# First scale and first gate of the modulation as dot products on VectorE instead of products on TensorE, in a one-core transformer kernel

## What is computed

```
sc   = silu(c)                                     # 1024 numbers
mod  = sc @ w_mod + b_mod                          # 6 vectors of 1024
sh1, s1, g1, sh2, s2, g2 = split(mod, 6)
h    = rms_norm(x, norm1_g) * (1 + s1) + sh1       # x: 256 tokens x 1024
u, gate = split(h @ w_pw1 + b_pw1, 2)
u    = dwconv(u * sigmoid(gate)) + b_dw            # width 31, in segments of 64 tokens
u    = silu(layer_norm(u)) @ w_pw2 + b_pw2
x    = x + g1 * u
x    = x + g2 * (relu((rms_norm(x) * (1 + s2) + sh2) @ w1)**2 @ w2)
...                                                # final norm, two attention layers
```

## Time and profile before

| | before |
|---|---|
| median of 3 runs | 1031.82 us (1031.65, 1031.82, 1034.67) |
| profiled execution, its own time | 1034.53 us |
| its span, first to last instruction | 1032.7 us |
| TensorE busy | 1002.6 us, 97% |
| VectorE busy | 603.2 us, 58% |
| ScalarE busy | 506.6 us, 49% |
| mean granted TensorE clock | 0.994 of full |

### The profile page before, as it was taken

The page is one execution under the profiler, slowest core; times in us unless marked ns, Lnnn a source line. Parts: engine busy times, 40 slices in busy tenths (PEclk is TensorE's granted clock), DMA queues, the critical chain, the costliest instruction groups (busy, mean ns, idle before and its releaser), DMA issues.

```text
span 1032.7 us, 13807 instructions
## 1 busy us (share of the span) xinstructions
PE 1002.6 (97%) x5782; PEld 843.5 (82%) x5782; DVE 603.2 (58%) x730; ACT 506.6 (49%) x639; POOL 23.7 (2%) x47
## 2 busy tenths in 40 slices
PE   8998999999998999999999999999999999999996
PEld 6665779999997999878888888889988788888885
DVE  3587355444447639955555455764796655545465
ACT  4443455444555545654444444554565643444453
POOL 0000000000000000000000000000000100000000
PEclk9999999999999999999999999999999999999998
DMA  9967597555505544046555555436233554555531
GB/s 344 418 254 285 212 379 255 214 186 188 211 22 191 215 145 164 27 155 221 200 182 185 202 172 211 165 126 236 90 115 123 176 210 175 203 171 196 191 115 42
DMA packets 30648, 195.57 MB, mean 189 GB/s; under 512 B 3571, under 2 KB 5672, under 8 KB 9592
## 3 DMA queue, kind: packets, MB, share of 16 engines
q1 hardware_dynamic: 30586, 194.68, 52.0%
HBM read 193.61 MB, written 2.04 MB: 189 GB/s over the span
## 4 chain that ended last, share of the span: by engine, by line
PE 82%; DVE 11%; issue 3%; ACT 3%; DMA 1%; POOL 0%; DVEq 0%; SPq 0%; POOLq 0%; ACTq 0%
PE ps L1593 58%; PE ps L1968 9%; PE ps L2024 5%; DVE lo L1048 3%; ACT hi L588 1%; PE ps L1698 1%; PE ps L2272 1%; PE ps L2154 1%; PE ps L2108 1%; DVE scratch L1385 1%; DVE scratch L1451 1%; PE ps L1715 1%; PE ps L1777 1%; DVE scratch L1402 1%; DMA h<-x 0%
## 5 line engine op out<-in xcount | busy, mean ns | idle before, releaser
L1048 DVE TENSOR_TENSOR lo<-raw,hi 128x2048 fp32r<-128x2048 f32 (+5 forms) x140 | 310.3, 2219 | 234.8 <-ACT hi L588 234.7
L588 ACT ACTIVATE hi<-raw 128x2048 fp32r<-128x2048 f32 (+4 forms) x140 | 263.8, 1888 | 127.0 <-PE ps L1593 105.5
L1593 PE MATMUL ps<-hi,xh 128*128 128x512 f32 (+2 forms) x704 | 276.3, 392 | 9.3 <-DVE xl L1089 4.3
L1593 PE MATMUL ps<-lo,xh 128*128 128x512 f32 (+2 forms) x704 | 269.7, 383 | 0.0
L1593 PE MATMUL ps<-hi,xl 128*128 128x512 f32 (+2 forms) x704 | 269.4, 383 | 0.0
L1593 PEld LDWEIGHTS ps<-hi,xh 128*128 128x128 f32 x704 | 132.4, 188 | 46.3 <-issue 14.2
L1593 PEld LDWEIGHTS ps<-lo,xh 128*128 128x128 f32 x704 | 132.4, 188 | 25.2
L1593 PEld LDWEIGHTS ps<-hi,xl 128*128 128x128 f32 x704 | 132.7, 189 | 22.3
L1593 PE MATMUL ps<-hi,gh 128*128 128x512 f32 (+2 forms) x328 | 125.1, 382 | 0.0
L1593 PE MATMUL ps<-lo,gh 128*128 128x512 f32 (+2 forms) x328 | 124.6, 380 | 0.0
L1593 PE MATMUL ps<-hi,gl 128*128 128x512 f32 (+2 forms) x328 | 124.6, 380 | 0.0
(11 more groups left out here) (248 smaller groups left out, 1063.2 us busy)
## 6 DMA issues: line engine op xcount, KB each, us to landing
raw<-stream SPq DMA_DIRECT2D x142, 1024.0 KB, 4.9
scratch<-stream SPq DMA_DIRECT2D x22, 1024.0 KB, 6.2
raw<-stream SPq DMA_DIRECT2D x4, 1020.0 KB, 4.9
raw<-stream SPq DMA_DIRECT2D x4, 896.0 KB, 5.9
raw<-stream SPq DMA_DIRECT2D x2, 864.0 KB, 4.5
raw<-stream SPq DMA_DIRECT2D x2, 768.0 KB, 4.5
raw<-stream SPq DMA_DIRECT2D x2, 680.0 KB, 5.0
h<-x SPq DMA_DIRECT2D x2, 512.0 KB, 4.5
```

The costliest lines, as they stand in the source:

```text
L588: nc.scalar.activation(hi[:, u["s"] % SPLIT_SLOTS, 0:n], raw_of(u, n), ACT.Copy).then_inc(S["hi_done"], 1)
L1048: nc.vector.tensor_tensor(lo[:, slot, first:n], raw_of(u, n)[:, first:n], hi[:, slot, first:n].bitcast(F32), ALU.subtract).then_inc(S["lo_ ...
L1593: ins = nc.tensor.matmul(out, l, r, start=start and i == 0, stop=stop and i == 2, skip_group_check=skip)
```

## The change

Two of the six vectors, `mod(0)` (first scale) and `mod(2)` (first gate), are now computed on VectorE alone. Their weights are laid out transposed in the stream, so that a partition holds the 1024 weights of one output channel; a unit holds two such blocks of 128 channels. `sc` stands as a row of 1024 on every partition (`crow`). For each block, one instruction multiplies weights by `crow` and sums along the row into one number per partition (`dots`). It writes its products back over the weights.

To make `crow`, VectorE spreads `sc` over eight diagonal blocks (`diagonals`, in the place of `stage`), TensorE multiplies them by a matrix of ones in two products of 512 columns ahead of the transposes, and ScalarE copies the 1024 columns.

For the scale, the dots give the columns directly: `columns` is split into `scale_columns` and `shift_columns`, and `quarters`, `quarter_copy` and half of `column_sums` disappear for `mod(0)`. For the gate, the eight columns are written to DRAM (4 KB) and read back as a row on all partitions; SP issues the write behind `pw2[3]` and waits for it, then issues the broadcast, and goes on with `mod(4,2)`. `row_sum` and the ScalarE copy of the row are gone for `mod(2)`. The `lo` of `pw2[1]` is moved from ahead of the second half's filter products to behind the normalisation of block 1. The slots of the dotted units are free when their two dots are done. Which unit stands where in the stream is not changed.

```
+DOTS = {(0, 0), (0, 1), (0, 2), (0, 3), (2, 0), (2, 1), (2, 2), (2, 3)}
...
-COLUMN_UNITS = ((0, 1), (2, 3), (4, 5), (6, 7), (12, 13), (14, 15), (16, 17), (18, 19))
+COLUMN_UNITS = ((None, 0), (None, 1), (None, 2), (None, 3), (4, 5), (6, 7), (8, 9), (10, 11))
...
@@ SP
-            end = units_of("w1", 1)[0]["index"]
+            end = units_of("pw2")[3]["index"] + 1
+            weights(UNITS[at:end])
+            sp.wait_ge(S["gate_done"], 1)
+            sp.dma_start(gate_dram.rearrange("(p j) -> p j", p=P), one["gate"]).then_inc(S["gate_dma"], 16)
+            sp.wait_ge(S["wave_ps"], CHUNKS)
+            sp.wait_ge(S["gate_dma"], 16)
+            sp.dma_start(one["g1"], gate_dram.partition_broadcast(P)).then_inc(S["gate_dma"], 16)
+            at, end = end, units_of("w1", 1)[0]["index"]
@@ ACT
+            act.wait_ge(S["xnT_ps"], 1)
+            nc.scalar.activation(crow, ps[:, 4:6, :].rearrange("p a c -> p (a c)"), ACT.Copy).then_inc(S["xnT_ready"], 1)
...
@@ DVE
+            nc.vector.tensor_tensor(diagonals, ident.rearrange("p (a m) -> p a m", a=1).broadcast_to([P, KT, P]),
+                                    vec[:, V_C:V_C + KT].rearrange("p (k a) -> p k a", a=1).broadcast_to([P, KT, P]),
+                                    ALU.mult).then_inc(S["sel_step"], 1)
...
+            def dots(v, q):
+
+                at = dotted(v, q)
+                u = DOT_UNITS[at // 2]
+                dve.wait_ge(landed[u["slot"]], u["landed"])
+                w = raw_of(u, SLOT).rearrange("p (i k) -> p i k", i=2)
+                for i in range(2):
+                    nc.vector.scalar_tensor_tensor(out=w[:, i, :], in0=w[:, i, :], scalar=1.0, in1=crow, op0=ALU.mult, op1=ALU.mult,
+                                                   accum_out=dot[:, at + i:at + i + 1]).then_inc(S["dot_done"], 1)
...
+                dots(0, i)
+                scale_columns(i)
                 if i == 0:
                     feed(units_of(("pw1", 0))[i], 0)
-                columns(i)
+                shift_columns(i)
...
-            partial_sums(0)
+            dots(2, 0)
             feed(units_of(("pw1", 1))[3], 0)
             dve.wait_ge(S["wave_done"], CHUNKS)
             filtered(0, 0, 1, 2, 3)
-            partial_sums(1)
+            dots(2, 1)
             feed(units_of("pw2")[0], 0)
             statistics(0, 0)
             statistics(0, 1)
-            partial_sums(2)
-            partial_sums(3)
+            dots(2, 2)
+            dots(2, 3)
...
             gated(1)
-            feed(units_of("pw2")[1], 0)
             filtered(1, 0, 1, 2, 3)
...
+            feed(units_of("pw2")[1], 0)
+            scale_columns(4)
+            shift_columns(4)
@@ PE
+            for i in range(2):
+                ins = nc.tensor.matmul(ps[:, 4 + i, :], one["ones"], one["stage"][:, i * CHUNK:(i + 1) * CHUNK], start=True, stop=True)
...
             for i in range(GROUPS):
-                if i < GROUPS - 1:
-
-                    pe.wait_ge(S["quarter_sb"], 2 * i + 1)
-                    quarters(2 * i + 2)
                 pw1_part(0, i, 0, (0,))
                 if i < GROUPS - 1:
-                    pe.wait_ge(S["quarter_sb"], 2 * i + 2)
-                    quarters(2 * i + 3)
+                    pe.wait_ge(S["quarter_sb"], i + 1)
+                    quarters(i + 1)
                 pw1_part(0, i, 0, (1,))
...
             pw1_part(1, 2, 0, (0, 1))
-            row_sum(0)
             used(pw1_part(1, 2, 1, (0, 1)), None)
-            row_sum(1)
             pw1_part(1, 3, 0, (0, 1))
-            row_sum(2)
             used(pw1_part(1, 3, 1, (0, 1)), None)
-            row_sum(3)
```

More of the change, by code:

```diff
@@ L153, in plan_units @@
     late = None
-    at, split, plain, landed, holder = 0, 0, 0, [0] * EARLY_SLOTS, [None] * EARLY_SLOTS
+    at, split, plain, dots, landed, holder = 0, 0, 0, 0, [0] * EARLY_SLOTS, [None] * EARLY_SLOTS
     for i, u in enumerate(units):
@@ L168, in plan_units @@
             split += 1
+        elif (u["stage"][1], u["n"]) in DOTS:
+            u["d"] = dots
+            dots += 1
         else:
@@ L323, in build @@
         rel_row = one["rel_row"][0:HD, :]
-        padded_taps = one["g2"][0:TAP_ROWS, :]
-        tap_rows = one["g2"][0:TAPS, :]
+        padded_taps = one["g1"][0:TAP_ROWS, :]
+        tap_rows = one["g1"][0:TAPS, :]
+        crow = one["crow"]
+        gate2 = one["crow"]
+        dot = one["dot"]
+        diagonals = one["stage"].rearrange("p (k m) -> p k m", k=KT)
         two = carve([("Z", 3072), ("X", 2304), ("Y", 2304), ("iqT", 4 * SEQ), ("ikT", SEQ), ("work", 3 * P),
@@ L754, in _ @@
                 if i == 0:
[L755 removed]
+                    row_copy(2, gate2)
                 if i == 1:
[L757 to L758 removed]
+                    quarter_copy(15)
+            row_copy(3, gate2)
             for j in range(MLP_CHUNKS):
@@ new lines, in shift_columns @@
+            def shift_columns(g):
+                ks = slice(GROUP_KT * g, GROUP_KT * (g + 1))
+                v, q = (1, g) if g < GROUPS else (3, g - GROUPS)
+                if (v, q) in DOTS:
+                    at = dotted(v, q)
+                    dve.wait_ge(S["dot_done"], at + 2)
+                    total = dot[:, at:at + 2]
+                else:
+                    dve.wait_ge(S["col_sums"], g + 1)
+                    bank, at = SUM_AT[g]
+                    total = ps[:, bank, at + GROUP_KT:at + 2 * GROUP_KT]
+                nc.vector.tensor_tensor(in_shift[:, ks], total, vec[:, V_SHIFT + ks.start:V_SHIFT + ks.stop],
+                                        ALU.add).then_inc(S["shift_done"], 1)
@@ L1175, in variance @@
                 nc.vector.tensor_scalar(ln_var[:, b:b + 1], ln_mv[:, b, 1:2], EPS, None, ALU.add).then_inc(S["ln_var"], 1)
-            steps = [0]
-            def partial_sums(r):
-                u = MODS[SPLIT_ROWS[r]]
-                dve.wait_ge(landed[u["slot"]], u["landed"])
-                w = raw_of(u, SLOT).rearrange("p (k c) -> p k c", k=KT)
-                dst = stage[:, SPLIT_ROWS[r] % 4, :]
-                nc.vector.tensor_scalar(dst, w[:, 0, :], vec[:, V_C:V_C + 1], None, ALU.mult).then_inc(S["partial"], 1)
-                for k in range(1, KT):
-                    steps[0] += 1
-                    dve.wait_ge(S["partial"], steps[0])
-                    ins = nc.vector.scalar_tensor_tensor(out=dst, in0=w[:, k, :], scalar=vec[:, V_C + k:V_C + k + 1], in1=dst,
-                                                         op0=ALU.mult, op1=ALU.add)
-                    ins.then_inc(S["partial"] if k < KT - 1 else S["partial_done"], 1)
             gated(0)
             feed(units_of(("pw1", 1))[2], 0)
-            partial_sums(0)
+            dots(2, 0)
             feed(units_of(("pw1", 1))[3], 0)
@@ L1203, in _ @@
             statistics(0, 1)
-            partial_sums(2)
-            partial_sums(3)
+            dots(2, 2)
+            dots(2, 3)
+            at = dotted(2, 0)
+            dve.wait_ge(S["dot_done"], dotted(2, 3) + 2)
+            nc.vector.tensor_tensor(one["gate"], dot[:, at:at + KT], vec[:, V_GATE:V_GATE + KT], ALU.add).then_inc(S["gate_done"], 1)
             dve.wait_ge(S["in_consts"], 32)
```

229 lines of the change are left out of this document (122 added, 107 removed).

## The result

| | before | changed |
|---|---|---|
| median (20 runs each) | 1033.65 us | 1035.18 us |
| lowest to highest | 1031.65 to 1036.2 | 1034.09 to 1037.6 |
| profiled execution, its own time | 1034.53 | 1036.29 |
| its span | 1032.7 | 1034.5 |
| mean granted TensorE clock | 0.994 | 0.988 |

The ratio is 1.0018, 95% interval [1.001, 1.0027]: 1.5 us slower on the medians, where 0.7 less was forecast (the median of before is now over 20 runs). The profiled executions differ by 1.8. All of that has arisen by 108 us: the second block of the second pointwise product starts at 108.62 (106.82 before), and the distance is the same 1.8 at the end. So the account closes ahead of the MLP.

The account below looks back on a forecast made before the run. TensorE, busy for 97% of the span, was taken as the bound. Terms +0.8 - 2.1 - 2.2 - 2.2 - 1.6 + 4.1 + 1.6 gave -1.6; weighed against +0.2, -0.7 on the median: 1031.1 us, range 1027.0 to 1035.5.

Parts of the forecast that it names:

- Start, +0.8: Up to group 0: the `crow` products and copy delay it, fewer column sums give some back; 0.8 us later in all.
- A dot pair, 2.6: On VectorE: two multiply-and-sum instructions of 1024 elements at 1.28 us each, 2.6 us a pair.
- Rival C: A summing dot on VectorE takes twice as long, 5.1 us a pair; total about +6.4, 1037.5 to 1038.2; chance 0.11.
- Groups, -2.1: First pointwise product's input groups: each sheds a `quarters` and half its column sums, partly lost to waits; 2.1 us gained.
- Row sums, -2.2: Between the products and beside the sigmoid's wait: four row sums of 0.43 + 0.31 go; 2.2 us gained.
- Moved `lo`, -2.2: Ahead of the second half's filters: they start at 84.7, not 90.42; 2.2 us, plus 1.6 from full clock in `tokens`.
- Where it goes back, +4.1 and +1.6: Ahead of the second pointwise product: TensorE waits 4.1 us for `mod(3,1)`, and the low clock behind it costs 1.6.
- The gate row's way, 0: Gate row through DRAM in SP's queue: `mod(4,2)` lands in time, cost 0, bounds 0 and +1.5 us.
- D: Single queue: gate's write lands late, TensorE waits 2 to 3 us at `quarters(8)`, second low clock; +3.5, near 1035; chance 0.14.
- A: As forecast: gains up to 91.3 us end at the wait for `mod(3,1)`; 1029.0 to 1033.4; chance 0.48.
- Rival B: Cheaper wait for `mod(3,1)`: clock stays up or load lands sooner; -3.2 down to -5, 1028.6 to 1026.8; chance 0.27.

Follow-up runs that it names:

- e1: Changed kernel with the `lo` of `pw2[1]` put back ahead of the filter products: 1031.05 us, ratio 0.9969 to the kernel before.
- e7: e3 with the loads of `mod(4,2)` and `mod(3,2)` issued ahead of the gate row's write: 1032.25 us, ratio 0.9989 to the kernel before.
- e4: Kernel before, with only the `lo` of `pw2[1]` moved behind the normalisation of block 1, no dots: 1038.75 us, ratio 1.0046.
- e3: Changed kernel with 16 unused products of ones where TensorE waits for `mod(3,1)`: 1033.53 us, ratio 0.9997 to the kernel before.
- e9: e8 with unused products of ones at the start, five behind the transposes, eight behind the first column sums: 1035.35 us, ratio 1.0008.
- e8: Kernel before, with only the `lo` of `pw2[1]` moved between the second half's gate products: 1032.83 us, ratio 0.9988.
- e6: e2 with unused products of ones in three gaps of TensorE's start: 1025.97 us, ratio 0.993 to the kernel before.
- e2: Changed kernel with the `lo` of `pw2[1]` between the second half's two gate products: 1028.47 us, ratio 0.9949 to the kernel before.
- e5: e2 with the first scale back on TensorE, only the gate dotted: 1030.3 us, ratio 0.9972 to the kernel before.

## Why the prediction was wrong

The sign of the forecast (-0.7) was wrong, at +1.5; the time lies inside the range. It was made against a median of three executions; over twenty the kernel before is 1.8 higher, at 1033.65. In the profiled times the forecast was -1.6 and +1.8 came: 3.4 between them.

- **Start, +0.8.** Wrong in size: +1.97. The two products took 1.97 for the 1.04 expected, at full clock: the row of `waves`, x2, is one product of 512 columns, and the prediction took it (and its lower bound of 0.86) as the price of two. Read rightly, the row gives 2.08. The copy took 1.03, and `open_pw1` came at 13.64 for 13.8, by luck: ScalarE's three copies ran from 10.64 to 13.51 without the 0.38 that it waited between two of them before. What was missing in the sum is the low clock over 16 to 20: `keep_busy` 2.23 instead of 1.76 and the quarter 1.91 instead of 1.04. The new products wait for the diagonals and `open_pw1` for three copies, and these gaps of TensorE were not weighed. Whether the clock falls there changes from execution to execution: e1 and e7, with the same start, kept it until 20 and 20.7, and lost it in or just behind the gap of 2.33 ahead of group 0.
- **A dot pair, 2.6.** Right. 16 dots, VectorE's groups with mean ns of one:

```profile
L1152 DVE SCALAR_TENSOR_TENSOR raw<-raw,scratch 128x1024 f32<-128x1024 f32 x16 | 18.9, 1221 | 0.7 <-issue 0.7
L1152 DVE DVE_READ_ACCUMULATOR raw<-raw,scratch 128x1 f32 x16 | 1.3, 84 | 0.0
```

  The sum along the row costs 0.08. Rival C is out: 1.22 with the sum against 1.28 without it is no halving. The rule that the prediction took from the Trainium skill's Vector Engine (DVE) Microarchitecture Reference, section Points that are easy to get wrong, does not hold for this instruction in the way the prediction applied it, as twice the time of the same form without the sum.
- **Groups, -2.1.** Right. Of the chain of waits before, this bullet and the row sums need:

```profile
56.65 1.13 PE ps L1742 x4
...
72.90 2.99 PE ps L1593 x12
...
76.63 2.94 PE ps L1593 x12
...
80.32 2.94 PE ps L1593 x12
...
84.00 2.96 PE ps L1593 x12
```

  From group 0 to the second `open_pw1` the changed kernel gained 1.97 + 0.12 = 2.1. The wait before group 1 was there, and hides what the lighter TensorE had to give.
- **Row sums, -2.2.** Too small by 0.7. The products ended at 83.95 instead of 86.96, which is 2.9 gained behind `open_pw1`. The three row sums between the products were 2.22; the last 48 products themselves took 11.83 in four pieces before and 11.16 in one piece now, so each break had cost 0.2 beside its own rows.
- **Moved `lo`, -2.2.** Right: filters at 85.21 (84.7 forecast), `tokens` at full clock, block 1 complete at 92.11 instead of 98.51, -6.4 for the 7.2 forecast. Of the 0.8 between them, 0.5 was there when the products ended (83.95 for 83.4): +1.2 from the start, less the 0.7 of the row sums.
- **Where it goes back, +4.1 and +1.6.** The step that failed, in its second half. The wait was 4.06 and the landing 4.86 for the 4.1 and 4.8 named. The low clock behind it cost 4.0 instead of 1.6. I had priced it like the two low stretches of before; this one lasted from 98 to 108, with TensorE without a gap from 99.34 on. +2.4 here and the 0.9 by which the quarter behind the wait came late (99.34 for 98.4: the 0.8 above and 0.1 in the landing) make the 3.4, to rounding. With the 1.6 of the prediction in place of the 4.0, the same execution would have been 0.6 faster than the one before: the sign hangs on this term; the start's +1.2 alone would not have turned it. How far the term holds beyond one execution is less sure, with 3.0 in e4 and 2.2 by the ratios in e3.
- **The gate row's way, 0.** Right for the changed kernel: write 6.7 and broadcast 4.4 to landing, not waited for. e3 shows that 0.5 becomes due once TensorE is 3 us ahead; D as a rival asked for 2 to 3.
- **The rivals.** A happened, with its clock term mis-sized, and ended 1.8 above its own range's 1033.4. Rival B's cheaper wait did not come in the two profiles that have the wait unfilled, the changed kernel and e4 (4.06 and 4.09, low clock in both). And a third way was missing from all of them: the `lo` had a place, between the gate products, where it cost neither stall. VectorE's idle time there was about to open, since 5.4 of work left the stretch ahead, and I had worked out that figure without asking where the idle time would fall.

Open: why the clock stayed low for 10 us in the changed kernel and for about 7 in e4 (0.59 and 0.56 granted over 100 to 104 and 104 to 108), behind a wait of the same length and with the same work following. What the rows add is when it fell: in the changed kernel at about 97.8, with 1.5 of the wait to go, in e4 at about 100.7, 0.4 ahead of the work at 101.14; it was back at about 108.1 and 107.6. Open too is why the clock of the start fell in some executions and not in others, and what made two loads of e9 late.

## What to carry to other kernels

When an instruction that frees a slot is moved, follow the slot to the load that waits for it and to the product that needs that load, and look first for idle time of its engine on the near side: in the kernel before, the same `lo` cost 0.46% behind the normalisation (e4) and saved 0.12% between the gate products (e8). A wait of TensorE costs its length and then the low clock behind it, which cost as much again in the changed kernel (4.06 and 4.0) and 3.0 behind 4.09 in e4; price it by the whole stretch that follows, and try unused products in the gap, but measure them: e3 with them was 2.2 us faster, e9 2.1 slower, by the ratios, and for e9 it is not shown that they are the cause. A saving that is early at the next load's door is not yet a saving: e6 kept it, e9 lost it.

## What was not expected of the hardware

The granted clock stayed at 0.50 from 98 to 108, though TensorE was never idle from 99.34 on. At the start it fell at about 16, behind two gaps much shorter than the 4.06, 7.13 to 8.65 and 12.35 to 13.64, in the changed kernel, e2 and e3. In e1, with gaps of 1.23 and 1.29 there, it did not, nor in e7, with 0.42 and 1.29, nor in e6, with 1.13 and 0.17. Ahead of group 0, almost the same gap had both outcomes: with 1.47 and 1.45 (before, e8) the clock fell to half, with 1.43 and 1.59 (e4, e5) it stayed full. One profile of a kernel is one draw of this. A write of 4 KB to DRAM, issued behind two loads of 1 MB, took 6.7 to land, and the read of it as a row on all partitions (512 KB) 4.4, where the load of 1 MB for `mod(3,1)` took 4.86:

```profile
scratch<-gate_dram SPq DMA_DIRECT2D x1, 512.0 KB, 4.4
gate_dram<-scratch SPq DMA_DIRECT2D x1, 4.0 KB, 6.7
```
